# Products that nobody reads, run by TensorE ahead of its waits, in an encoder kernel of six stages per layer

## The reference

```
h = rmsnorm(x, norm_g[l])
proj = jnp.einsum('bsd,de->bse', h, w_in[l])
o_a = windowed_gqa(...)          # 8 heads, window of 128
o_b = diff_attention(...)        # 4 heads, softmax minus lam times softmax, all 1024 keys
o_fwd, o_bwd = gated_delta_chunked(...)   # 4 heads, chunks of 64, both directions
merged = gates[0] * y_a + gates[1] * y_b + gates[2] * y_c
x = x + jnp.einsum('bsd,de->bse', merged, w_out[l])
```

## Time and profile before

| | us |
|---|---|
| median of 3 runs | 3485.57 |
| lowest and highest of them | 3480.43, 3488.3 |
| span of the profiled execution | 3476.7 |

### The profile page before, as it was taken

One profiled execution on the slowest core, in us unless ns is written; L12 is line 12 of the kernel. 1 busy time (PEld: TensorE's weight loads), 2 busy tenths in 40 slices (PEclk: granted clock), 3 DMA queues, 4 the chain that ended last, 5 costly groups with the idle time before them and its releaser, 6 DMA issues. The chain is left out here.

```text
span 3476.7 us, 42840 instructions
## 1 busy us (share of the span) xinstructions
PE 2906.6 (84%) x15946; PEld 2389.4 (69%) x15946; DVE 1804.9 (52%) x2187; ACT 1134.9 (33%) x1867; POOL 1167.1 (34%) x500
## 2 busy tenths in 40 slices
PE   4979797898968986989978898888887888788996
PEld 2858686677746775867757676766665666687775
DVE  6126465556548833347331555565554874523653
ACT  2113132555534422331111222245444353133311
POOL 2432322223325541036344323222322555211551
PEclk9989897999989998999989998999998999889997
DMA  4232322212224434564322323132221544356542
GB/s 141 79 103 74 91 72 87 82 57 84 90 91 159 162 115 135 149 227 133 127 77 91 97 67 97 63 96 70 74 84 54 170 152 141 108 157 199 168 136 103
DMA packets 403196, 388.30 MB, mean 112 GB/s; under 512 B 91232, under 2 KB 341728, under 8 KB 403040
## 3 DMA queue, kind: packets, MB, share of 16 engines
q1 hardware_dynamic: 364832, 300.26, 29.7%
q10 hardware_dynamic: 38208, 85.99, 6.4%
HBM read 253.99 MB, written 132.19 MB: 111 GB/s over the span
## 5 line engine op out<-in xcount | busy, mean ns | idle before, releaser
L200 PE MATMUL pair<-h_hi,w_hi 128*128 128x512 f32 x1792 | 755.2, 421 | 172.6 <-PEq L132 79.8
L200 PE MATMUL pair<-h_lo,w_hi 128*128 128x512 f32 x1792 | 724.5, 404 | 0.0
L200 PE MATMUL pair<-h_hi,w_lo 128*128 128x512 f32 x1792 | 720.9, 402 | 0.0
L200 PEld LDWEIGHTS pair<-h_hi,w_hi 128*128 128x128 f32 x1792 | 354.8, 198 | 292.8 <-SPq L130 83.4
L184 POOL TENSOR_TENSOR w_hi<-w_stage,masks 128x1024 fp32r<-128x1024 f32 x108 | 285.6, 2644 | 729.9 <-PE pair L200 513.6
L200 PEld LDWEIGHTS pair<-h_lo,w_hi 128*128 128x128 f32 x1792 | 354.7, 198 | 75.5 <-issue 5.7
L200 PEld LDWEIGHTS pair<-h_hi,w_lo 128*128 128x128 f32 x1792 | 352.1, 196 | 78.7
L186 POOL TENSOR_TENSOR w_lo<-w_stage,w_hi 128x1024 fp32r<-128x1024 f32 x108 | 281.1, 2603 | 8.5
L215 ACT ACTIVATE ev<-pair 128x512 f32<-128x512 f32 x224 | 132.2, 591 | 424.3 <-PE pair L200 424.3
L153 PE MATMUL pair<-h_hi,w_hi 128*128 128x512 f32 x576 | 183.3, 400 | 39.8 <-DVE h_lo L537 27.5
L1093 ACT ACTIVATE diff_p<-pair,diff_stat 128x1024 f32<-128x1024 f32 x128 | 143.0, 1117 | 206.9 <-DVE diff_stat L1166 202.7
(11 more groups left out here) (281 smaller groups left out, 5762.9 us busy)
## 6 DMA issues: line engine op xcount, KB each, us to landing
w_stage<-in_w_in SPq DMA_DIRECT2D x132, 512.0 KB, 5.3
proj<-ev ACTq DMA_DIRECT2D x132, 512.0 KB, 2.6
gate<-proj SPq DMA_DIRECT2D x48, 512.0 KB, 3.4
prep_x<-proj SPq DMA_DIRECT2D x24, 512.0 KB, 3.5
diff_vx<-proj SPq DMA_DIRECT2D x18, 512.0 KB, 4.6
diff_xr<-proj SPq DMA_DIRECT2D x72, 128.0 KB, 3.9
prep_g<-gc_rows SPq DMA_DIRECT2D x16, 512.0 KB, 4.2
qd_t<-prep_eg SPq DMA_DIRECT2D x16, 512.0 KB, 2.6
```

The lines of the kernel that those rows point to most:

```text
L200: last = nc.tensor.matmul(bank(self.banks[half]), a[s][:, c, :], b[:, c, w], start=(c == 0 and n == 0), stop=(c == KC - 1 and n == 2))
```

## The change

A helper `keep_on` issues `count` fp32r matmuls of one and the same pair of operands (128x128 weights, 128x512 moving) into a PSUM bank whose content nobody needs any more. It is called in eight places of PE's stream: as the last work of each stage (project 28, window 24, full 56, prepare 34, delta 48, merge 44), and twice in each head of full: 16 behind the transposition of v, after a wait until the first side half is copied out, and 24 ahead of the waits of the last transposition. In prepare there is also a wait for `qm`. No other engine's code is touched, and nothing is removed.

```diff
+        def keep_on(pe, into, count):
+            for _ in range(count):
+                nc.tensor.matmul(into, h_hi[:, 0, 0:P], h_hi[:, 0, 0:HALF], start=True, stop=True)
@@ project, end of PE's stream
                         units(i)
+                    keep_on(pe, bank(4), 28)
@@ attend_window, end
                                 last.then_inc(q["summed"], 1)
+                    keep_on(pe, bank(0), 24)
@@ attend_full, in each head
                         last.then_inc(q["v_turned"], 1)
+                        pe.wait_ge(q["side_out"], START + h * 8 + 1)
+                        keep_on(pe, bank(7), 16)
                         pe.wait_ge(q["lo"], START + 2 * h + 2)
...
                                 m = t - 1
+                                if t == NT:
+                                    pe.wait_ge(q["side_out"], START + h * 8 + 7)
+                                    keep_on(pe, bank(7), 24)
                                 pe.wait_ge(q["mixed"], START + NT * h + m + 1)
@@ attend_full, end
                         last.then_inc(q["total"], 1)
+                    keep_on(pe, bank(0), 56)
@@ prepare, end
                         half(7)
+                    pe.wait_ge(q["qm"], START + 8)
+                    keep_on(pe, bank(2), 34)
@@ delta_rule, end
                             side_half(next(sides))
+                    keep_on(pe, bank(0), 48)
@@ merge_output, end
                                 last.then_inc(q["total"], 1)
+                    keep_on(pe, bank(6), 44)
```

## The result

The changed kernel takes 3500.26 us (median of 7 runs, 3495.49 to 3505.91); the kernel before, run beside it, 3488.3 (7 runs, 3480.43 to 3493.69). The ratio is 1.0037, with a 95% interval of 1.0026 to 1.0048: slower, by 9 to 17 us, which is about a third of a percent. I had forecast 3503 and +17.8. Every run's span lies some 2 us under its time, and the profile of after is of a run near its median (span 3501.2).

A forecast was written before the change was run, and what follows sets the result against it. PE's work plus PE's waits were taken as the bound. Terms 44.8 - 6.6 - 15.2 - 10.8 + 5.6 = +17.8 us, added to the median 3485.6, gave 3503 us; range 3486 to 3530.

The forecast's parts named there:

- The barrier follows PE's products: Stage ends: PE's drain waits for the products, so the barrier's release moves later; 22.4 us a layer, +44.8 us in all.
- The clock behind the barrier comes back in part: Behind stage ends: less work at the low clock, final sum included; -6.6 us together, bounds 0 and -21.
- The final sum: Behind the last merge: the four-part sum, 3.75 us at clock 0.50, should take half, saving 1.8 us.
- a third: Behind project, window and full: a third of the possible 2.5, 2.1 and 2.5 us comes back, 2.4 us a layer.
- The condition I set for being wrong: Stages behind a 3 us gap beginning at clock 1.00 throughout would show the prediction wrong.
- The heads give back: Heads of full: less waiting and low clock make a later head shorter by 3.7 us (1.9 and 1.8).
- The last transposition: Full, 8 times: 24 products fit in the wait and the clock stays up behind it; -15.2 us, bounds 0 and -16.
- scores of heads 1 to 3: Full, 6 head starts: scores begin 1.1 us later but regain 2.9 us of low clock; -1.8 each, -10.8 us.
- Full, head 0, twice: Full's first head in each layer: products start late at a low clock and delay the scores; +2.8 us each, +5.6.
- 1: Heads of full: they give nothing back, PE works at 0.50 from the head's start; 23 us more, 3526; chance 0.20.
- 3: Stage ends: the barrier is not held up by the products, the 44.8 nearly vanish; -47 us, 3439; chance 0.07.
- Rival 2: Stage ends: the clock holds across the barrier, giving back 21 us instead of 6.6; +3.4, 3489; chance 0.19.
- Rival 4: Whole change: the build drops or merges the products and nothing changes; given no chance.

The follow-up runs named there:

- the three runs on the other chip: Products only ahead of the last transposition 3461.38 us, only at head starts 3474.12, only at head starts without the copy wait 3462.65; each against the kernel before.
- the first two experiments: Changed kernel with products only at the six stage ends, 3523.77 us; then only in the two head calls, 3457.78 us; against the kernel before +39.5 and -26.5.

## Why the prediction was right, point by point

- **The barrier follows PE's products.** Shown, at every stage end and by the dose (96, 48, 14, 0 products behind delta: 31.7, 20.9, 13.3, 13.2 us). The terms of the earlier trace rows: project 1.3 forecast, 1.4 measured; window 4.5, 4.2 and 4.7; full 0.5, 0.6; prepare 2.8, 2.8; delta 7.5, 7.8; the second merge 5.8, 5.8. The first merge came to 7.0 instead of 5.8. Over both layers 46.9 instead of 44.8. The release of the barrier follows PE's drain by 0.1 us at all twelve, as I had said.
- **The clock behind the barrier comes back in part.** Stage ends alone cost 39.5 with ways longer by 46.2, so 6.7 came back, where 6.6 was forecast; the interval (33 to 44) does not hold that number tightly. The clock of all fourteen profiles bears it out better. Over the 5 us behind project the ten stage ends with products ran at 0.66 to 1.00, in the mean at 0.73, the eighteen without at 0.50 to 0.70, in the mean at 0.58; behind full it is 0.73 against 0.53; behind window 0.59 against 0.58. At full clock that is 0.8, 1.0 and less than 0.1 us of work a layer, where I had taken 0.8, 0.8 and 0.7. The final sum takes 1.96 us in place of 3.75, 1.8 as forecast. Together that makes 5.5 us over both layers, an estimate. No single stage shows "a third": of the twenty ends of project and full with products four are followed by 1.00 and sixteen by 0.66 to 0.68, behind gaps of 3.1 to 3.4 us in both kinds. The 2.5 us that I took as lost behind project held for the first profile (0.50 in both layers), not for the second (0.65 in layer 1). The condition I set for being wrong, all stages behind 3 us gaps at 1.00, did not occur.
- **The heads give back.** A later head is shorter by 3.3 to 4.0 us (98.6 against 101.9 and 102.3 and, in the second profile of before, 102.6 and 102.5); 3.7 was forecast. The last transposition took 0.83 us of wait in place of 6.29 and its 4.0 us at 1.00, and scores of heads 1 to 3 began at 1.00, 5.5 us behind the transposition of v instead of 4.3: 1.2 us later, 1.1 forecast. Head 0 of layer 1, from full's start to its last transposition, is 101.8, 103.2 and 101.7 us long in the three profiles with the products that wait for the copy, against 99.1 to 101.6 (mean 100.2) in the seven with nothing at its start; in layer 2 it is 100.1, 101.1 and 102.7 against 98.7 to 100.8 (mean 99.9). So it is 2.0 and 1.4 us dearer, 3.5 together before rounding, where 2.8 each was forecast.
- **The size.** The +17.8 of the forecast lies just outside the interval (+9 to +17). The part that was off is the heads: -20.4 forecast, -26.5 by the medians and -23.7 by full's length. The term that was sized worst is "Full, head 0, twice", +5.6 where the traces show +3.5; with it the forecast's own steps make -22.5. The 1.2 us from there to full's length are within its scatter of 3; the 2.8 from full's length to the medians, like the 4 to 6 in the three runs on the other chip, are not accounted for.
- **The rivals.** 1 and 3 fell with the first two experiments. The Trainium skill (TensorE: Matmul & The Clock Gate, "Part 4: PE-mode transpose") has transpositions not count as busy; here the clock was at 1.00 behind eight of them and a wait of 1.69 us (the 16 products took 3.92 us), at all 18 starts of later heads with these products, which does not contradict the page, since matmuls stood in front. Rival 2 fell with the stage ends alone: in the changed kernel the clock held behind project and full of layer 2, not of layer 1, and in that run behind none of them. Rival 4 fell with the count of matmuls, 788 more.
- **The baseline.** I added the difference to the median and not to the lucky span; that step kept the forecast (3503) near the 3500 measured. That it came within 3 us is in part luck: the difference was forecast 5.8 us too high (+17.8, not +12.0), and the median of three runs that I added it to was 2.7 us under that of the seven (3485.6, 3488.3).

## What to carry to other kernels

A wait on the profile is two things, the part that a barrier has yet to collect and the part that begins only when it has; filler in front of the barrier may use the first alone, and only up to the moment when the slowest other engine reports. Put it ahead of a wait that another engine's chain ends (the last transposition), count it to end just short of that release, and give it a target that needs no wait of its own. And when a change puts the same trick in eight places, run the places apart: +39.5 and -26.5 looked like a harmless +12.

## What was not expected of the hardware

- The same program's profiled executions differ by 12.3 us (3476.7 and 3489.0), as much as the whole effect; a sum made on one trace needs the spread of the others beside it.
- The way from merge to project with no product at merge's end is 11.1 to 12.7 us, by run (seven profiles). A part of that is SP's chain: its 35 semaphore instructions of L130 take 2.6 us in the kernel before, 3.3 in the changed kernel and 3.6 with heads alone, in this order, where nothing of SP's code differs:

```profile
L130 SPq EVENT_SEMAPHORE  x35: 17/17/17, 1741.7 to 1744.3; - x35
```

```profile
L130 SPq EVENT_SEMAPHORE  x35: 17/17/17, 1754.0 to 1757.3; - x35
```

```profile
L130 SPq EVENT_SEMAPHORE  x35: 17/17/17, 1732.9 to 1736.5; - x35
```

  Each takes 17 ns, so the time lies between them. PE's first matmul of project's sums comes 8.0 us behind the release in the changed kernel (1749.7 to 1757.67) and 6.9 in the kernel before; that 1.1 us is what merge's 7.0 has over the 5.8 forecast, and 0.7 of it lies in this chain. Among the fourteen profiles the chain takes 2.5 to 2.7 us in three (both of before, and the head starts with their wait alone) and 2.9 to 3.6 in the eleven others. Why it does was not tried.
